# Gate and branch products of a finished branch issued inside the next branch's norms, rotations, attention and recurrence

## The reference

```python
h = rmsnorm(x, ln_mix[l])
z = h @ w_in[l]          # 2848 columns for four mixers, then 4 x 1024 gate logits
o_mla, o_fnet, o_diff, o_hgrn = ...   # each 512 x 256
merged = 0
for n, o_branch in enumerate((o_mla, o_fnet, o_diff, o_hgrn)):
    gate = sigmoid(gate_logits[..., n * 1024:(n + 1) * 1024])
    merged = merged + gate * (o_branch @ w_branch[l, n])
x = x + merged @ w_out[l]
x = x + (silu(h2 @ w_gate) * (h2 @ w_up)) @ w_down[l]     # h2 = rmsnorm(x, ln_ffn[l])
```

## Time and profile before

| what | us |
|---|---|
| median of 3 runs | 4270.31 (4269.96 to 4271.09) |
| the profiled execution's own time | 4269.49 |
| span in its profile, first to last instruction | 4267.3 |
| first mixer stage, start of its first matmul to start of its output product | 1943.93 to 2680.68 |
| second mixer stage, likewise | 3105.08 to 3839.85 |

### The profile page before, as it was taken

The page is one execution under the profiler, slowest core; times in us unless marked ns, Lnnn a source line. Parts: engine busy times, 40 slices in busy tenths (PEclk is TensorE's granted clock), DMA queues, the critical chain, the costliest instruction groups (busy, mean ns, idle before and its releaser), DMA issues.

```text
span 4267.3 us, 44857 instructions
## 1 busy us (share of the span) xinstructions
PE 3885.6 (91%) x16532; PEld 3026.5 (71%) x16532; DVE 1920.9 (45%) x2669; ACT 1342.4 (31%) x2020; POOL 144.0 (3%) x106
## 2 busy tenths in 40 slices
PE   6999599999999999998787799899987777999999
PEld 5888488878877778885355578788853455877887
DVE  6642766333335543323544744433235546444332
ACT  3222322232225542323333222322233332223221
POOL 1000200000000000000100000000001000000000
PEclk8999799999999999999878599999998786999999
DMA  7743277323331223333011033233320010332332
GB/s 260 244 122 93 95 252 231 93 88 95 95 93 55 60 65 98 92 96 87 5 30 50 1 85 99 79 98 93 99 72 15 20 50 1 99 98 79 94 95 88
DMA packets 626890, 390.83 MB, mean 92 GB/s; under 512 B 17088, under 2 KB 584256, under 8 KB 625600
## 3 DMA queue, kind: packets, MB, share of 16 engines
q1 hardware_dynamic: 621376, 376.82, 29.8%
q10 hardware_dynamic: 5376, 12.14, 0.8%
HBM read 386.81 MB, written 2.10 MB: 91 GB/s over the span
## 4 chain that ended last, share of the span: by engine, by line
PE 81%; DVE 9%; ACT 4%; issue 3%; DMA 1%; POOL 1%; ACTq 0%; SPq 0%; DVEq 0%; POOLq 0%
PE bank L1823 22%; PE bank L1824 22%; PE bank L1825 22%; PE bank L1982 2%; DVE ada_acc L1164 1%; PE bank L1838 1%; DMA work<-in_ada_w 1%; ACT w_hi L680 1%; PE bank L1930 1%; PE bank L1839 1%; PE bank L1840 1%; PE bank L2069 1%; PE bank L1849 1%; PE bank L2075 1%; PE bank L1974 1%
## 5 line engine op out<-in xcount | busy, mean ns | idle before, releaser
L1147 DVE TENSOR_TENSOR w_lo<-stage,w_hi 128x1024 fp32r<-128x1024 f32 x587 | 720.2, 1227 | 1734.5 <-ACT w_hi L680 1734.4
L1823 PE MATMUL bank<-h_hi,w_hi 128*128 128x512 f32 x3064 | 1210.5, 395 | 45.5 <-DVE h_lo L1399 29.8
L1825 PE MATMUL bank<-h_hi,w_lo 128*128 128x512 f32 x3064 | 1200.8, 392 | 0.0
L1824 PE MATMUL bank<-h_lo,w_hi 128*128 128x512 f32 x3064 | 1200.1, 392 | 0.0
L680 ACT ACTIVATE w_hi<-stage 128x1024 fp32r<-128x1024 f32 x587 | 621.7, 1059 | 1755.5 <-PE bank L1825 1667.7
L1823 PEld LDWEIGHTS bank<-h_hi,w_hi 128*128 128x128 f32 x3064 | 579.8, 189 | 177.0 <-DVE h_lo L1399 32.5
L1824 PEld LDWEIGHTS bank<-h_lo,w_hi 128*128 128x128 f32 x3064 | 580.2, 189 | 123.4 <-issue 3.4
L1825 PEld LDWEIGHTS bank<-h_hi,w_lo 128*128 128x128 f32 x3064 | 579.7, 189 | 121.5
L1825 PE MATMUL bank<-a_hi,w_lo 128*128 128x512 f32 x1056 | 410.8, 389 | 0.0
L1823 PE MATMUL bank<-a_hi,w_hi 128*128 128x512 f32 x1056 | 410.8, 389 | 0.0
L1824 PE MATMUL bank<-a_lo,w_hi 128*128 128x512 f32 x1056 | 410.8, 389 | 0.0
(11 more groups left out here) (255 smaller groups left out, 3654.5 us busy)
## 6 DMA issues: line engine op xcount, KB each, us to landing
stage<-in_ffn_w_in SPq DMA_DIRECT2D x176, 512.0 KB, 3.8
stage<-in_w_in SPq DMA_DIRECT2D x108, 512.0 KB, 3.8
stage<-in_w_gate_up SPq DMA_DIRECT2D x88, 512.0 KB, 3.7
ada_stage<-in_ada_w SPq DMA_DIRECT2D x128, 256.0 KB, 4.5
work<-in_ada_w SPq DMA_DIRECT2D x128, 256.0 KB, 6.1
stage<-in_ffn_w_out SPq DMA_DIRECT2D x64, 512.0 KB, 3.5
stage<-in_w_down SPq DMA_DIRECT2D x32, 512.0 KB, 3.7
stage<-in_ffn_w_out SPq DMA_DIRECT2D x32, 384.0 KB, 3.0
```

The source lines that it names most:

```text
L1147: nc.vector.tensor_tensor(w_lo[:, w * WORDS:(w + 1) * WORDS], stage[:, slot * WORDS:(slot + 1) * WORDS], w_hi[:, w * WORDS:(w + 1) * WORDS ...
L1823: nc.tensor.matmul(dst, wh, chunk(hi, k), start=first and a == 0, stop=False)
L1824: nc.tensor.matmul(dst, wh, chunk(lo, k), start=False, stop=False)
L1825: ins = nc.tensor.matmul(dst, wl, chunk(hi, k), start=False, stop=last and a == len(ks) - 1)
```

## The change

The merge loop is dissolved. A piece of work called a fill, `fill(f)` with f from 0 to 31 in a layer, is one gate unit (24 matmuls into bank 6) and one branch product for the same 128 output channels (6 matmuls into bank 7, weights loaded as a block of 256x128 by `branch_load`, with their own high and low tiles in the statistics region). The branches are taken in the order fnet, mla, diff, hgrn. Fills 0 to 7 (fnet) stand in the mla norms, rotations and attention, fills 8 to 15 (mla) in the diff ones, fills 16 to 23 (diff) in the recurrence, and fills 24 to 31 (hgrn) follow one another at the end.

Per fill, ACT loads the table set `exp_and_others` if it isn't there, makes the high branch weights (128x256), takes tanh(x/2) of the gate in place of the sigmoid, and converts the high part of the unit two ahead; DVE makes the low branch weights (128x256), then waits for the branch product, computes (tanh + 1) * branch in one instruction, and makes the low part of the unit two ahead. For f of 8 and more POOL adds the result to the merged tile; the missing factor of one half is applied when the merged tiles are split (`merged_high`, `merged_low`). That split is now done tile by tile between the last fills.

To free banks 6 and 7, scores use three banks (0 to 2) and head outputs bank 3, norms two banks (4, 5) in place of four; rotations get four banks (0 to 3) in place of two, and level scores alternate between banks 0, 1 and 2, 3. In the recurrence the two heads of a pair alternate matmul by matmul on PE (in scores and in the products with the values) where one head used to follow the other; ACT copies the scores of levels 0 and 1 in two portions, and issues level 0's exponentials of the second pair ahead of the first pair's outputs. Squares of the mla latents and the diff inputs are issued between the projections, and token-major transposes of hgrn's values too. `fox_head` and the causal variant, which nothing used, are gone.

```diff
+            def fill(f):                                   # ACT
+                rel, g = MIX_UNIT["gate", f], n.merge + f
+                nc.scalar.preload_act_table_set("exp_and_others")
+                branch_high(f)
+                act.wait_ge(unit_done, n.unit + rel + 1)
...
+                nc.scalar.activation(gs[:], bank[6][:], ACT.Tanh, scale=0.5).then_inc(sig_ready, 1)
+                convert(rel + 2)
...
+            def fill(f):                                   # DVE
+                g = n.merge + f
+                branch_low(f)
+                dve.wait_ge(sig_ready, g + 1)
+                dve.wait_ge(wb_done, g + 1)
+                nc.vector.scalar_tensor_tensor(wk(MERGED + f) if f < DC else gs[:], gs[:], 1.0, bank[7][:], ALU.add,
+                                               ALU.mult).then_inc(gated_ready, 1)
+                next_weights("gate", f)
...
+            def fill(l, f):                                # PE
+                gate(f)
+                branch(l, f)
...
                 scores(0)
+                fill(l, fills)
                 for h in range(len(heads)):
                     if h + 1 < len(heads):
                         scores(h + 1)
                     outputs(h)
+                    if h + 1 < len(heads):
+                        fill(l, fills + h + 1)
...
-                ropes(mla_ropes)
+                ropes(mla_ropes, 0, 4)
+                fill(l, MLA_FILL + 2)
+                ropes(mla_ropes, 4, 8)
+                fill(l, MLA_FILL + 3)
...
+                    if lv in fills:
+                        fill(l, fills[lv])
+                fill(l, (H_FILL + 4, H_FILL + 6)[p])
+                pe.wait_ge(hcopied, 24 * pair + 24)
+                for c in range(TB):
                     for hp in range(2):
...
-                looped(pe, 2, step)
...
+                gate(H_FILL + 7, 0, 4)
+                stats(hgrn_norms(l))
+                gate(H_FILL + 7, 4, DC)
+                branch(l, H_FILL + 7)
+                for d in range(DC):
+                    fill(l, H_DENSE + d)
...
+MLA_FILL, DIFF_FILL, H_FILL, H_DENSE = 0, 8, 16, 24
+H_FILL_AT = ({3: 18, 6: 19}, {4: 21})
```

More of the change, by code:

```diff
@@ L86, in __init__ @@
         self.merge = 0
+        self.zbase = 0
         self.level = 0
@@ L576, in fox @@
+                n.unit += len(MIX_UNITS)
+                n.merge += MERGES
             def fox():
@@ L1384, in attention @@
                     copies(h)
+                    if h + 1 < len(heads):
+                        weights(h + 1)
+                        fill(fills + h + 1)
                 n.block += TB * mp * len(heads)
@@ L1592, in mix @@
+                fill(DIFF_FILL + 7)
+                splits([wk(DIFF_O + c) for c in range(2)], 2)
+                for c in range(8):
+                    next_weights("hgrn", c)
+                n.z += 8 + TB
                 dve.wait_ge(z_ready, n.z)
```

819 lines of the change are left out of this document (443 added, 376 removed).

## The result

The changed kernel took 4119.05 us (median of 4 runs, 4113.76 to 4119.91), the kernel before beside it 4270.24 us: ratio 0.9642, 95% interval 0.9629 to 0.9654. That is 151 us less, where 233 less (4036) were forecast: 34 us above the forecast's own range (3995 to 4085), and 9 above the wider 3970 to 4110 that it also gave. The direction was right, a third of the gain was not there.

The account below looks back on a forecast made before the run. PE was 91% busy, so only its lost time in five mixer parts could be won. Terms of -3.4, +16.6, +7, +11, +21.5, -167.4 and -2 gave -116.7 us a layer, -233.4 in all: 4036 us, range 3995 to 4085.

Parts of the forecast that it names:

- The end: Layer end: 223.7 us becomes 8 dense fills, 54.8, plus 1.5 for a split; the 4.39 us wait goes; -167.4 us a layer.
- The recurrence: 8 fills in the 127 us recurrence, where DVE sets the pace at 3.98 us a level: +21.5 us a layer.
- fill 20: Recurrence, at the pair's end: fill and value products fit into PE's 14.9 us before the exponentials of level 1, -1.3 us.
- near 205: Sign in the later profile: time from the last hgrn projection to the output product, near 205 us.
- The price of a fill: Each fill: 6.85 us of PE at full clock, 2.3 of DVE, some 2.3 of ACT, and a POOL addition holding DVE about 1.
- the sign: What would show the forecast wrong: PE waiting for w_lo or wb_lo in the fills because weights come late.
- Diff attention: 5 fills in the 88 us diff attention: first head 14.8, three of 21.5; +11 us a layer.
- plus 4 for scores that still run at the lower clock: Diff attention: 4 us a layer added to 95 for score matmuls still below the full clock.
- POOL's additions: 24 additions a layer; one can hold DVE by about 1 us, bounds 0 and 1.1, charged where DVE sets the pace.
- Mla attention: 4 fills, 27.4 us, in a 52 us part with 16 us free: grows to 68.6, +16.6 us a layer.
- The clock stays low: Rival: all 13 fills in recurrence and diff attention run at 1.2 GHz, 6.0 us more each; 4196 us; chance 0.11.
- Slower: Rival: DVE's in-order queue waits in each fill; without overlap each lengthens its part by 9.2 us; 4367 us; chance 0.03.

Follow-up runs that it names:

- the added matmuls: Changed kernel plus 6 unused 512-column matmuls ahead of the scores of each recurrence level from the fourth on: 4115.34 us.
- the weights ahead: Changed kernel with each fill's branch weights converted at the end of the fill before: 4116.08 us.
- The dense kernel: Changed kernel with no fill inside another branch's work, each branch's 8 run together after the next branch's attention or recurrence: 4229.57 us.
- the trace without the additions: Changed kernel with GpSimd's additions of merged branches cut to 8 of 512 columns: 4107.12 us.
- The edits: Changed kernel with branch weights made a fill ahead and gate product deferred only where each helped, tanh table loaded 6 times a layer: 4078.81 us.
- 128 rows: Diff scores read from all 128 rows of their tiles instead of each map's 32, against the kernel of "The edits": 4052.89 us.

## Why the forecast missed, step by step

**Right.** The end: 54.4 us for 56.3, no wait before the output product. The recurrence: 149.9 for 148.5, though partly by luck. By the starts of its scores the three fills behind levels cost 4.5, 3.1 and 4.7 us beyond three periods of 3.98, for the 5 each; what fill 20 and the shorter waits for copies gave back was 5.9 us for the 9.6 counted. (The "about 4 us" that a fill was to take to the full clock are 4.8 in the row it was read from; the gate products behind levels ran 1.7 to 1.9 us longer than dense ones, near the 2 that it took.) Its level's period stayed 3.98 us, as in the earlier trace rows; one after the other in the changed kernel:

```profile
3523.43 2.08 PE L2164 MATMUL bank<-work 64*128 64x128 f32 x16 [1.99 <-DVE work L1583]
...
3527.41 0.80 PE L2164 MATMUL bank<-work 64*128 64x128 f32 x4 [1.90 <-DVE work L1583]
```

That VectorE and not the clock sets that pace was shown by the added matmuls. From fill 16's first gate product, behind the last projection, to the output product, 3694.14, it is 204.2 us for "near 205". That the gain is limited by what the parts can hold, and not by the 164 us moved, was right in kind.

**The price of a fill: the failed step.** It charged VectorE 2.3 us a fill as work to be added to its queue ("DVE needs 8 x 2.04 + 2 x 2.3 = 20.9"), and let only VectorE wait for TensorE. In the program the low weights stand at the fill's own place, behind the rotations, and they need ScalarE's high part, which stands behind its splits and the table load. So TensorE waits in turn, the rotations took 34.4 us for the 24 forecast, and where the earlier trace rows had TensorE wait once for VectorE, the lines above have waits of 5.62, 1.04 and 3.16 us. Placing the weights and the gate product where they don't stand in the way gave 34 us; the 1.28 us table load, for which the forecast had no term (ScalarE's "some 2.3 us too" are a conversion, a copy and a tanh), gave 14 alone and about 6 on top. Together 40 us. Not all of it lies where the forecast missed: by the table some 16 us a layer are in the norms, rotations and attentions, the rest in the projections behind diff attention and at the end. Of the mla rotations' 10.4 us the weights ahead gave back 7.5. The forecast had named the sign and the cause among what would make it wrong, but gave them no term and no rival.
The same sum also took the busy time of a chain for its period: the earlier trace rows has 24.6 us for 8 rotations, 3.07 each, where 3 x 0.68 = 2.04 was used. The dense kernel has 23.5 us for the same eight and shows that period nearly unchanged; so with no fill in them at all the rotations take what the forecast gave them with two.

**Diff attention.** The step "plus 4 for scores that still run at the lower clock" was mis-sized. The first head was 18.0 us for 14.8, the next 24.97 and 25.70 for 21.5, the first 9 scores 0.23 us apart and nearly all of the other 15, behind the wait, 0.43:

```profile
3340.98 0.49 PE L2061 MATMUL bank<-extra_r,work_r 32*128 32x512 f32 x1
...
3342.69 0.38 PE L2062 MATMUL bank<-work_r 32*128 32x512 f32 x1
3342.91 0.38 PE L2063 MATMUL bank<-extra_r,work_r 32*128 32x512 f32 x1
3344.46 0.50 PE L2061 MATMUL bank<-extra_r,work_r 32*128 32x512 f32 x1 [1.16 <-ACT work L837]
...
3346.15 0.62 PE L2063 MATMUL bank<-extra_r,work_r 32*128 32x512 f32 x1
3346.57 0.62 PE L2061 MATMUL bank<-extra_r,work_r 32*128 32x512 f32 x1
...
3365.95 0.49 PE L2061 MATMUL bank<-extra_r,work_r 32*128 32x512 f32 x1
```

Taking the 32-row products away gave 26 us in the whole, and 10.3 a layer in this part, against the 4 a layer charged: some 6 us a layer of the miss, 13 in both. The forecast held that the fills' dense work would keep the clock; it did so for the fills, not for the scores behind them.

**POOL's additions.** The sum charged 1 us at each of fills 17, 18, 19 and 21, 4 a layer; the trace without the additions has 4.2 less. The size was right and the place was not: 0.6 of it is in the recurrence.

**Mla attention.** The first scores with their fill took 11.3 us for 9.7, the three heads 20.7, 18.6 and 18.7 for 17.7 each, the last outputs 6.4 for 5.8: the 7.1 us. Four fills hid 3.2 us, since the part's own matmuls already filled most of its 51.5. The edits made it 71.9 for the 68.6 forecast.

**The rivals.** "The clock stays low" (4196) held that all 13 fills of diff attention and recurrence run 6.0 us longer; the ones behind scores at the lower level ran 1.4 to 1.9 us longer, the others did not, and the rows cost 10.3 us in diff attention, a small part of its 80 a layer. Transposes did not lower the clock: with 128 rows it read 1.00 across a head's 16. "Slower" held that a fill adds its full price wherever it stands: nearly true of the diff norms, where 3.3 of 20.6 us were hidden, false of the sum. None of the four had TensorE wait for weights. What is left open: of the 45 us a layer that the four parts missed, the edits took back some 16 and the rows explain 6 more. The other 23 a layer are not shown: 9 of them lie in the diff norms, where the clock reads 0.81 and the rotations' period was also taken too short, the rest in the first heads and the chain of the norms; no run took them apart.

## What to carry to other kernels

Work that is interleaved costs more than its length on the busiest engine: follow each of its small helpers (a conversion, a table load) through the in-order queue of the engine that makes it, and ask who waits at that place. An edit that moves such helpers can help in one stage and harm in the next by the same amount, so a run that shows no difference is read stage by stage before the theory is dropped. Measure a chain's period from starts in the trace, never as the sum of its instructions.

## What the hardware showed that I had not expected

The granted clock of the diff attention read 0.82 with score products of 32 rows and 0.98 with 128 rows, with as many products and columns and a longer wait ahead of them. Why, no run here shows. A load of the table that is active already costs the same 1283 ns as a change: all 64 loads of the changed kernel's fills took that, 52 of them needless. Products in different groups of rows issued in turn overlap: 16 of 64 rows and 128 columns took 2.08 us at the lower clock where one group after the other took 3.06, both at a granted clock of 0.50. The Trainium skill, "TensorEngine Tiling (Array Packing)", section "When to Use Tiling", advises packing the array by rows for contractions of 64 rows or fewer; the trace agrees, and six products of 32 rows took 1.65 us for 2.6; yet the kernel with them was 14 us slower, and its pairs waited 1.17 us each for ScalarE.
